# DeltaNet steps: keys, normed output and values turned by VectorE and through memory instead of TensorE; sums of squares by ScalarE

## The reference

```
h = rmsnorm(x);  proj = h @ w_in            # 9232 columns
o_r = retention(rq, rk, rv)                 # 4 heads, chunks of 128
q, k, v = silu(causal_conv(dq, dk, dv))     # 4 taps
o_d = gated_deltanet(l2norm(q), l2norm(k), v, beta, g)   # 8 heads of 128 columns
o_d = o_d * rsqrt(mean(o_d * o_d) + eps) * dn_g;  o_d = o_d * silu(dz)
x = x + (sigmoid(gr) * (o_r @ w_up_r) + sigmoid(gd) * (o_d @ w_up_d)) @ w_o
```

## Time and profile before

| | us |
|---|---|
| median of three executions | 2646.9 |
| span of the profiled execution | 2644.2 |
| TensorE busy | 2620.6 |
| VectorE busy | 1761.1 |
| ScalarE busy | 704.5 |
| GpSimd busy | 798.6 |

### The profile page before, as it was taken

How to read it: one execution, slowest core, us unless ns; L and a number is a source line. 1 busy time by engine, 2 the same in 40 slices (tenths; PEclk the granted TensorE clock), 3 DMA queues, 4 the chain that set the end, 5 groups by cost and what they waited for, 6 DMA issues and landing times.

```text
span 2644.2 us, 40210 instructions
## 1 busy us (share of the span) xinstructions
PE 2620.6 (99%) x14874; PEld 2238.1 (85%) x14874; DVE 1761.1 (67%) x3972; ACT 704.5 (27%) x1440; POOL 798.6 (30%) x451
## 2 busy tenths in 40 slices
PE   8999999999999999999999999999999999999998
PEld 6888888888888899888877888888888998898887
DVE  7878777877755555434577778777877555653333
ACT  5333333333311212200143333333332221231001
POOL 3123333333312212334512233332322122132453
PEclk9999999999999999999999999999999999999999
DMA  5321222122211112433533222222222111133344
GB/s 174 100 85 58 81 69 85 53 86 65 85 50 43 41 35 76 130 96 120 157 90 88 77 74 69 73 77 72 67 77 73 43 51 43 41 106 100 99 135 152
DMA packets 293416, 217.79 MB, mean 82 GB/s; under 512 B 31747, under 2 KB 246101, under 8 KB 292965
## 3 DMA queue, kind: packets, MB, share of 16 engines
q1 hardware_dynamic: 259620, 159.07, 20.9%
q10 hardware_dynamic: 33600, 56.15, 6.3%
HBM read 176.30 MB, written 38.86 MB: 81 GB/s over the span
## 4 chain that ended last, share of the span: by engine, by line
PE 92%; DVE 3%; DMA 2%; issue 1%; ACT 1%; SPq 0%; POOL 0%; ACTq 0%; DVEq 0%; POOLq 0%
PE dense_ps L866 23%; PE dense_ps L870 23%; PE dense_ps L868 23%; PE work L849 3%; PE dense_ps L890 2%; PE dense_ps L891 2%; PE dense_ps L892 2%; PE work L1145 1%; PE work L1182 1%; PE work L1202 1%; PE work L1121 1%; PE work L1104 1%; PE work L1171 1%; PE work L1195 1%; PE work L1156 1%
## 5 line engine op out<-in xcount | busy, mean ns | idle before, releaser
L866 PE MATMUL dense_ps<-act_hi,w_hi 128*128 128x512 f32 x2552 | 1048.3, 411 | 1.7 <-DVE w_lo L1797 0.8
L870 PE MATMUL dense_ps<-act_hi,w_lo 128*128 128x512 f32 x2552 | 998.4, 391 | 0.0
L868 PE MATMUL dense_ps<-act_lo,w_hi 128*128 128x512 f32 x2552 | 997.3, 391 | 0.0
L2579 POOL TENSOR_TENSOR w_lo<-w_raw,w_hi 128x1024 fp32r<-128x1024 f32 x162 | 400.1, 2470 | 1024.5 <-ACT w_hi L1429 582.7
L870 PEld LDWEIGHTS dense_ps<-act_hi,w_lo 128*128 128x128 f32 x2552 | 479.0, 188 | 105.8
L866 PEld LDWEIGHTS dense_ps<-act_hi,w_hi 128*128 128x128 f32 x2552 | 481.0, 188 | 86.9 <-POOL act_lo L2600 2.3
L868 PEld LDWEIGHTS dense_ps<-act_lo,w_hi 128*128 128x128 f32 x2552 | 481.5, 189 | 78.8 <-issue 0.5
L1973 DVE SCALAR_TENSOR_TENSOR arena<-arena,cols 128x512 f32<-128x512 f32 x288 | 244.3, 848 | 6.1
L1429 ACT ACTIVATE w_hi<-w_raw 128x1024 fp32r<-128x1024 f32 x94 | 99.1, 1054 | 330.5 <-PE dense_ps L870 310.5
L1419 ACT ACTIVATE arena<-dense_ps 128x512 f32<-128x512 f32 x96 | 57.2, 596 | 258.5 <-PE dense_ps L870 258.5
L849 PE MATMUL work<-mk,arena 128*128 128x128 f32 x768 | 112.1, 275 | 7.9 <-DMA arena<-in_x 7.9
(11 more groups left out here) (262 smaller groups left out, 4094.7 us busy)
## 6 DMA issues: line engine op xcount, KB each, us to landing
w_raw<-in_w_in SPq DMA_DIRECT2D x138, 512.0 KB, 3.8
arena<-l_scratch SPq DMA_DIRECT2D x64, 256.0 KB
arena<-gate_scratch ACTq DMA_DIRECT2D x64, 256.0 KB, 2.7
gate_scratch<-arena ACTq DMA_DIRECT2D x36, 256.0 KB, 2.0
w_raw<-in_w_out SPq DMA_DIRECT2D x18, 512.0 KB, 3.7
o_scratch<-arena ACTq DMA_DIRECT2D x32, 256.0 KB, 2.2
w_raw<-in_w_up_dn SPq DMA_DIRECT2D x16, 512.0 KB, 3.6
arena<-o_scratch ACTq DMA_DIRECT2D x32, 256.0 KB, 3.7
```

Of the source, the lines that this page charges most:

```text
L866: eng.matmul(dense_ps[:, to, :], w_hi[:, slot, k, :], hi[:, k, seg], start=(k == 0), stop=False)
L868: eng.matmul(dense_ps[:, to, :], w_hi[:, slot, k, :], lo[:, k, seg], start=False, stop=False)
L870: mm = eng.matmul(dense_ps[:, to, :], w_lo[:, slot, k, :], hi[:, k, seg], start=False, stop=(k == KT - 1))
L2579: eng.tensor_tensor(w_lo[:, slot, :, :], w_from[second][:, :, :], w_hi[:, slot, :, :].bitcast(F32), ALU.subtract)\
```

## The change

In the seven even and seven odd units of a layer, TensorE turns neither the normed output nor the values, and in all of them but even units of head 0 not the keys either. VectorE turns blocks of 32x32 within 512 columns instead (`turn_o`, `turn_v`, `turn_k`, slots 15 to 17) into `turned`; ScalarE's queue writes them to memory in four transfers of 32 partitions each (`put_v`, slot 16, `put`, slot 18), so that the blocks of one 128x128 tile come to stand in turned order, and reads them back with tokens on the partitions into `tokens` (`get_v`, slot 19, `get`, slot 21). The values have transfers of their own. The values' product vt moves from slot 19 to slot 23. The gated output of a unit is made in slot 3 of the next one (`late_ob`) and stored in its slot 10 (`late_store`). The keys turned in a unit are those which the next one's kt reads. In odd units of head 6 turn_k does nothing. `turned` and `tokens` lie where the retention later has its rotated keys and queries. The sums of squares of queries and outputs are made by ScalarE's activations with an accumulated output, one for each chunk, and VectorE's two reductions are gone. Some semaphores are joined to make room for the new ones. The core of the diff:

```diff
 HBUF = 4
+BACK = 3
+BACK_O, BACK_K, BACK_V = range(BACK)
...
         at(13, "og")
         if kind.endswith("last"):
             at(16, "ob")
-        at(18, "store")
+            at(18, "store")
+        if kind in ("even", "odd"):
+            at(3, "late_ob")
+            at(10, "late_store")
+        elif kind == "even_last":
+            at(1, "late_ob")
+            at(3, "late_store")
...
-        at(vt, "vt")
+        at(23 if kind in ("even", "odd") else vt, "vt")
...
     if kind in ("even", "odd"):
         at(12, "mask", 1)
         at(14, "dec", 1)
-        begin(15, 1, ("ob",))
+        begin(15, 1, ("turn_o",))
+        at(16, "turn_v")
+        at(16, "put_v")
+        at(19, "get_v")
+        at(17, "turn_k")
+        at(18, "put")
+        at(21, "get")
...
+        turned = arena[:, swap_at:swap_at + BACK * HALF].rearrange("p (m s) -> p m s", s=32)
+        tokens = arena[:, swap_at + BACK * HALF:swap_at + 2 * BACK * HALF].rearrange("p (x c t) -> p x c t", x=BACK, c=CPH)
...
+        back_dram = nc.dram_tensor("back_scratch", [CPH * CPH * BACK, 32, P], F32)
...
                         elif what == "kt":
 
+                            if kind == "odd" or kind == "even" and h:
+                                continue
...
                         elif what == "vt":
 
+                            if kind in ("even", "odd"):
+                                continue
...
                         elif what == "ob":
-                            eng.wait_ge(on_ok.sem, on_ok.after(t, 1))
-                            turn(1 + b, [on[:, c, :] for c in range(CPH)]).then_inc(ob_ps.sem, 1)
+                            eng.wait_ge(on_ok.sem, on_ok.after(t, BACK + 1))
+                            turn(1 + b, [on[:, c, :] for c in range(CPH)]).then_inc(back_ps.sem, 1)
...
-                            if t is not None:
-                                eng.wait_ge(og_s.sem, og_s.after(t, 0))
-                            eng.activation(sq, wk[1 + nb][:, :], ACT.Square).then_inc(sq_ok.sem, 1)
+                            eng.wait_ge(qe_s.sem, qe_s.after(tn, 0))
+                            for c in range(CPH):
+                                ins = eng.activation(sq[:, c * P:(c + 1) * P], wk[1 + nb][:, c * P:(c + 1) * P], ACT.Square,
+                                                     accum_out=qss[:, c:c + 1])
+                            ins.then_inc(sq_ok.sem, 1)
...
                         elif what == "osq":
                             eng.wait_ge(o_ps.sem, o_ps.after(t, CPH))
-                            if kind != "odd_last":
-                                eng.wait_ge(qe_s.sem, qe_s.after(tn, 1))
-                            eng.activation(osq, wk[1 + b][:, :], ACT.Square).then_inc(osq_ok.sem, 1)
+                            eng.wait_ge(og_s.sem, og_s.after(t, 0))
+                            for c in range(CPH):
+                                ins = eng.activation(osq[:, c * P:(c + 1) * P], wk[1 + b][:, c * P:(c + 1) * P], ACT.Square,
+                                                     accum_out=og[:, 0, c:c + 1])
+                            ins.then_inc(osq_ok.sem, 1)
+                        elif what == "put_v":
+                            u = back(l, h, b)
+                            ms = slice(BACK_V * CPH * CPH, (BACK_V + 1) * CPH * CPH)
+                            eng.wait_ge(on_ok.sem, on_ok.after(t, 3))
+                            eng.wait_ge(back_v_in.sem, back_v_in.after(u, 0))
+                            for i in range(CPH):
+                                rows = slice(32 * i, 32 * i + 32)
+                                eng.dma_start(back_dram[ms, :, rows].rearrange("m r s -> r m s"), turned[rows, ms, :])\
+                                   .then_inc(back_v_st.sem, 16)
+                        elif what == "get_v":
+                            u = back(l, h, b)
+                            ms = slice(BACK_V * CPH * CPH, (BACK_V + 1) * CPH * CPH)
+                            eng.wait_ge(back_v_st.sem, back_v_st.after(u, 64))
+                            eng.wait_ge(vb_ok.sem, vb_ok.after(tn, 0))
+                            eng.dma_start(tokens[:, BACK_V], back_dram[ms, :, :].rearrange("(m j) r d -> (j r) m d", j=CPH))\
+                               .then_inc(back_v_in.sem, 16)
+                        elif what == "put":
+                            u = back(l, h, b)
+                            ms = slice(0, 2 * CPH * CPH)
+                            eng.wait_ge(on_ok.sem, on_ok.after(t, BACK + 1))
+                            eng.wait_ge(back_in.sem, back_in.after(u, 0))
+                            for i in range(CPH):
+                                rows = slice(32 * i, 32 * i + 32)
+                                eng.dma_start(back_dram[ms, :, rows].rearrange("m r s -> r m s"), turned[rows, ms, :])\
+                                   .then_inc(back_st.sem, 16)
+                        elif what == "get":
+                            u = back(l, h, b)
+                            eng.wait_ge(back_st.sem, back_st.after(u, 64))
+                            eng.wait_ge(kd_ok.sem, kd_ok.after(tn, 1))
+                            eng.wait_ge(ob_ok.sem, ob_ok.after(t, 0))
+                            eng.dma_start(tokens[:, 0:2].rearrange("p x c t -> p (x c) t"),
+                                          back_dram[0:2 * CPH * CPH, :, :].rearrange("(m j) r d -> (j r) m d", j=CPH))\
+                               .then_inc(back_in.sem, 16)
+                        elif what == "late_store":
+                            if kind == "even" and h == 0:
+                                continue
+                            seg = slice(nb * HALF, (nb + 1) * HALF)
+                            eng.wait_ge(ob_ok.sem, ob_ok.after(t - 1, 1))
+                            eng.dma_start(o_dram[bass.ds(h - nb, 1), :, seg].rearrange("k p t -> p (k t)"), sz[:, seg])\
+                               .then_inc(o_st[nb].sem, 16)
...
+                    elif old is not None and old % (2 * DH) == 0:
+                        eng.wait_ge(back_ps.sem, back_ps.after(l, 1))
                     elif old is not None:
-                        eng.wait_ge(vt_ps.sem, vt_ps.after(old, 1))
+                        eng.wait_ge(on_ok.sem, on_ok.after(old - 1, 3))
...
-                            eng.wait_ge(kt_ps.sem, kt_ps.after(tn, 1))
+                            if kind == "odd" or kind == "even" and h:
+                                eng.wait_ge(back_in.sem, back_in.after(back(l, h, b) - 1, 16))
+                                src = tokens[:, BACK_K]
+                            else:
+                                eng.wait_ge(kt_ps.sem, kt_ps.after(3 * l + ("first", "even", "even_last").index(kind), 1))
+                                src = chunks(4)
...
-                            eng.tensor_tensor(kd[nb], chunks(4), per_token(hs[:, 3, ns_of]), ALU.mult).then_inc(kd_ok.sem, 1)
+                            eng.tensor_tensor(kd[nb], src, per_token(hs[:, 3, ns_of]), ALU.mult).then_inc(kd_ok.sem, 1)
...
-                            eng.tensor_reduce(qss, sq.rearrange("p (c t) -> p c t", c=CPH), mybir.AxisListType.X, ALU.add)\
-                               .then_inc(qe_s.sem, 1)
-                            eng.wait_ge(qe_s.sem, qe_s.after(tn, 1))
...
                         elif what == "vt":
-                            eng.wait_ge(vt_ps.sem, vt_ps.after(tn, 1))
+                            if kind in ("even", "odd"):
+                                eng.wait_ge(back_v_in.sem, back_v_in.after(back(l, h, b), 16))
+                                src = tokens[:, BACK_V]
+                            else:
+                                eng.wait_ge(back_ps.sem, back_ps.after(l, 1 if kind == "first" else 3))
+                                src = chunks(0)
...
                             eng.wait_ge(vs_ok.sem, vs_ok.after(tn, 1))
-                            eng.tensor_tensor(vb[nb], chunks(0), per_token(ky[:, 5, :]), ALU.mult).then_inc(vb_ok.sem, 1)
+                            eng.tensor_tensor(vb[nb], src, per_token(ky[:, 5, :]), ALU.mult).then_inc(vb_ok.sem, 1)
...
-                            eng.tensor_reduce(og[:, 0, :], osq.rearrange("p (c t) -> p c t", c=CPH), mybir.AxisListType.X,
-                                              ALU.add).then_inc(og_s.sem, 1)
-                            eng.wait_ge(og_s.sem, og_s.after(t, 1))
-                            eng.wait_ge(qe_s.sem, qe_s.after(t, 2))
+                            eng.wait_ge(qe_s.sem, qe_s.after(t, 1))
...
+                        elif what == "turn_o":
+                            eng.wait_ge(on_ok.sem, on_ok.after(t, 1))
+                            eng.transpose(turned_of(BACK_O), on.rearrange("p c t -> p (c t)")).then_inc(on_ok.sem, 1)
+                        elif what == "turn_v":
+                            eng.wait_ge(kqv_ok.sem, kqv_ok.after(hn, 5 + nb))
```

(16 more changed lines are left out.)

43 lines of the change are left out of this document (29 added, 14 removed).

## The result

The changed kernel takes 2765.5 us (median of four executions, 2759.2 to 2766.6), the kernel before 2645.6 on the same chip: 1.045 times as long (95% interval 1.044 to 1.046), 120 us more. The forecast was 2665 us with 2687 as its upper end: the sign is right, the size is not. The profiled execution took 2765.3 us and spans 2763.4.

A forecast was written before the change was run, and what follows sets the result against it. TensorE, busy 99%, was taken to bound the kernel. Each pair gained +2.4 us of even-unit lateness less 1.15 saved in the odd unit, +1.3; 14 pairs, +18 on 2646.9, gave 2665 us, forecast's own range 2643 to 2687, overall 2614 to 2687.

The forecast's parts named there:

- the stall at vt: TensorE waits at ks_0 of odd units for vt, moved behind the even unit's last silu: 3.5 us, 14 times.
- rival 1: At the even unit's end VectorE finishes vt in time, so the whole 31.5 us saving shows: 2615 us; chance 0.23.
- the prices on VectorE and ScalarE: Per unit, block turns of 0.69 us on VectorE; sums cost ScalarE 0.8 us more, delaying nothing.
- the first term without a row: A 128x512 block turn on VectorE, a size no profile row showed: 0.69 us, with 0.48 and 1.2 as ends.
- 0.9 us worse off, as reckoned: Even unit's end: GpSimd's later low part holds VectorE's filter taps, +0.9 us (0 to 1.1).
- A turn's price on TensorE: Four transposes: 0.36 us for an output or key turn, 0.43 for a value turn; 31.5 us over both layers.
- SP's chain ... comes 1.8 us later; the solve of the next unit starts 2.4 us later itself.: Weight load, solve's stores and loads, behind GpSimd's low part, come 1.8 us later, covered by the next solve's 2.4 us.
- the 2.3 us that TensorE was to save in a pair: Turns removed from TensorE in an even and an odd unit: 1.15 us in each ordinary unit.
- Rival 2: Small packets cost 31 ns, put lands late, ScalarE stands at get: +81 us, 2728 us; chance 0.12.
- my place for this rival, the tanh: Even unit's end: ScalarE stands at get with the second queries' tanh behind it; vt ends at 676.9, unit grows 5.1 us.

The follow-up runs named there:

- early_even: Whole change, but in even units the values' block turn, stores and load stand in slots 2, 5 and 8, and vt in slot 19: 2720.2 us, 1.028.
- sums_only: Kernel before the change with only the two sums of squares moved to ScalarE: 2646.4 us, 1.000.
- split_first: Changed kernel with put_v one slot later (17), behind ScalarE's weight split: 2753.1 us, 1.040.
- early_even_split: Whole change with the even units' values turned, stored and loaded early, vt there in slot 19, and the odd units' put_v behind the weight split: 2680.2 us, 1.013.
- key_traffic: Kernel with only the output through memory, plus the keys' block turn, stores and load, read by nobody: 2654.0 us, 1.0032.
- values_pe: Changed kernel with the values turned by TensorE again; keys and output still through memory: 2659.3 us, 1.0046.
- key_src_sbuf: Kernel with only the output through memory, with kt's product reading unturned keys in SBUF in 26 units: 2634.3 us, 0.996.
- output_only: Changed kernel with values and keys turned by TensorE; only the normed output through memory, sums on ScalarE: 2632.1 us, 0.994.
- keys_later: Kernel with keys and output through memory, values by TensorE, with the odd units' kt in slot 4 instead of 2: 2658.7 us, 1.005.
- mended_keys_pe: Whole change with keys by TensorE, the even units' values early and the odd units' put_v behind the weight split: 2631.2 us, 0.995.
- mended_v2: mended_keys_pe with the even units' last silu moved behind the odd unit's first uu: 2629.1 us, 0.994.

## Why the prediction was right in sign and wrong in size

**Right: the stall at vt.** Forecast 3.5 us at ks_0 of the odd units, 14 times; measured 48.3 / 14 = 3.45. That vt went "from slot 19 to slot 23, behind that last silu" is its cause: with the even units' values early and vt back in slot 19 it vanishes (early_even), and 45 us with it. This also decides rival 1: VectorE was not in time. The sign isn't luck either: in the pair above the first stall and the clock behind it outweigh all that TensorE saved, by 3.2 us.

**Right: the prices on VectorE and ScalarE.** The block turns, the first term without a row, took what I had chosen between 0.48 and 1.2. The end of the even unit above, VectorE and GpSimd:

```profile
621.30 0.69 DVE L2435 STREAM_TRANSPOSE arena<-arena 128x512 f32<-128x512 f32 x1
...
622.39 4.34 DVE L2051 SCALAR_TENSOR_TENSOR arena<-arena,cols 128x512 f32<-128x512 f32 x3
622.47 2.93 POOL L2693 TENSOR_TENSOR w_lo<-w_raw,w_hi 128x1024 fp32r<-128x1024 f32 x1 [2.80 <-ACT w_hi L1463]
...
630.67 0.69 DVE L2067 SCALAR_TENSOR_TENSOR arena<-arena 128x512 f32<-128x512 f32 x1 [0.69 <-ACT arena L1469]
631.27 0.68 DVE L2322 TENSOR_TENSOR arena<-arena 128x512 f32<-128x512 f32 x1
```

The three taps at 622.39 take 4.34 us beside GpSimd's low part; three of them took 2.33 before (665.21), where one tap of 1.62 stood ahead of them for 0.48, so they are 0.9 us worse off, as reckoned. The last tap ends 27.1 us behind ks_3 where it ended 26.1 behind it before, 1.0 later; I had 0.8. Over the run a tap's mean went from 0.85 to 1.07 us. vt follows the silu without a wait for its rows (over the run 3.1 us in 9 waits): get_v was in time. The sums on ScalarE cost nothing (sums_only). A turn's price on TensorE came out at 0.43 where I had 0.36 for the output's.

**Wrong: "SP's chain ... comes 1.8 us later; the solve of the next unit starts 2.4 us later itself."** This is the step that missed the second stall. It is true for the next unit only if that is an odd one, which has the stall at ks_0 in front of it. For an even unit, behind an odd one without a stall, TensorE comes earlier, not later, and nothing covers the delay. I had walked SP's chain for one kind of unit and let it stand for both. What the runs show in its place is a second stall, 38.2 us in 12 waits and 7.0 in 2 at L1229, with the clock behind it; it goes with put_v behind the split (split_first, early_even_split). The size was short too. Against the next ks_1, the eight stores stand 7.9 us ahead (575.46 to 583.35) where they stood 11.2 ahead before (710.25 to 721.4), 3.3 later; the loads stand 1.1 us ahead (582.27) in place of 6.2 (715.17). Four issues of put_v at 0.4 to 0.5 us were about right: they take 2.0 us in the median, 2.32 in this unit. But I gave the solve's stores no delay from put and put_v, whose packets precede them; they land after 3.4 us and not 2.1. In key_traffic, where a delay of this kind stands alone, it costs 22 us.

**Wrong: the clock had no price.** "The granted clock should stay at its upper level; if stalls lower it, all terms grow" stood under what would show it, and no term or rival had it. In the pair above it adds 1.2 us behind the first stall and 2.7 behind the second; of the growth around the second 0.45 us is not assigned.

**The sum again.** Per pair of the profile above, against before: +3.4 and -0.7 from ks_3 to ks_0 of the odd unit (29.15 against 26.5), +1.2 behind it; -0.7 from ks_3 of the odd unit to ks_1 of the even one; +4.45 and +2.7 around the second stall (3.43 of stall, 0.57 at xu_1, 2.7 clock). That is 10.35, against 98.8 - 88.5 = 10.3. Of the 2.3 us that TensorE was to save in a pair 1.4 can be seen here; in the pairs in which ks_3 of the odd unit to ks_1 of the even one takes 30.24 us (31.57 before) it is 2.1. Fourteen such pairs would be 144 us; but this one is the longest, the fourteen grew by 8.4 us on average, and that makes 117 of the 120.

**Rival 2, small packets, is answered by halves.** The queue that carries the new transfers had this before:

```profile
q10 hardware_dynamic: 33600, 56.15, 6.3%
```

and this after:

```profile
q10 hardware_dynamic: 253120, 100.20, 13.6%
```

These are 219,520 packets more for 3350 us of one engine's time (13.6% of 16 x 2763 less 6.3% of 16 x 2644), 15 ns each; with the forecast's 31 ns for the 43,008 of 512 B that the loads make (28 x 1024 and 28 x 512), about 12 are left for one of 128 B, as taken. ScalarE issued get_v at 573.69, 0.1 us behind put's last store, and didn't stand there; my place for this rival, the tanh, was wrong. But its core, that the burst delays somebody, was right: the one delayed is SP's chain of 4 KB stores.

**Left open.** That the product of the keys, which reads SBUF now, is held is seen (2.07 us at 582.14, 0.69 before), beside GpSimd's low part of 581.27 to 583.65. The Trainium skill (SBUF — State Buffer, Who interferes with whom) says that a VectorE instruction with two SBUF inputs, as this one, contends with a GpSimd instruction that reads SBUF, and that one with a single SBUF input, outside the fast modes, doesn't. The traces agree on both: in values_pe all 26 block turns of the keys lie wholly beside GpSimd's low part and take 0.69 to 0.70 us. The prediction could show that for the taps alone. What the held product costs by itself no run shows: in key_src_sbuf it was held by 0.4 us only. Between values_pe and output_only lie 27 us. key_traffic's 22 us of packets were measured with TensorE still turning the keys; in values_pe it doesn't, which at the forecast's 0.36 saves 9. So 27 + 9 - 22 = 14 us are not assigned. The place where most of them may lie is ks_1 to ks_2 of the odd units, 6.5 us in values_pe against 5.7, in all 11: the keys' product is held there (1.5 us), but keys_later, in which it isn't (0.68), got only 0.3 of the 0.8 us back. Turning the keys early, as the values, wasn't tried.

## What to carry to other kernels

When work is moved to a queue, follow every chain that hangs behind it to its last consumer, and do it for each kind of iteration: cover that a stall gives in one kind is missing in the other. Transfers that nobody waits for still cost if they are issued in a burst right ahead of small ones that somebody does; the same number of bytes in smaller stores and partly at another time was free here. A stall of TensorE is to be priced with the clock behind it, here up to 2.7 us on one of 3.4.

## What the hardware showed that I had not expected

The length of a stall doesn't decide alone whether the clock falls. Behind 3.37 us (533.23) it fell, for about 3.4 us; around the end of 3.43 us (593.50) it was at 0.56 on average for seven. In the same run it fell at a stall of 2.38 us (397.86) and stayed at 1.00 at stalls of 2.47 (1958.31) and 2.94 us (2054.29); in early_even it fell behind 2.46 us. The kernel before has one stall of 2.9 us, in the second layer, and there the clock stayed up too. The three stretches are the one behind 397.86 and the one behind 1958.31, both after, and the one behind 1415.60, before:

```profile
397.86:401.00 3.14, 3.14 (x9) 2.56 (x10) 2.26 (x12) 0.00 (x0) 0.00 (x0) 0.50 0.00 0
1958.31:1962.00 3.69, 3.69 (x22) 3.29 (x23) 2.96 (x14) 0.28 (x1) 0.00 (x0) 1.00 0.00 0
...
1415.00:1417.00 2.00, 1.40 (x7) 1.26 (x8) 1.83 (x10) 0.00 (x0) 0.00 (x0) 1.00 0.02 4
```

The other surprise is how little the three turns cost one by one, and how much they do at one place. The values' way was free with the even units' part early and the odd units' stores behind the split (2631.2 us, all values through memory), the output's way gained 12 us, and the keys' block turn was free; with all of them in slots 16 to 21, 120 us were lost. The reverse holds too: spread, the values' way gave back only 1 us of the 12 that TensorE's rows promise for 28 turns. The steps of mended_keys_pe against those of output_only, on average over the 14 pairs, say where the rest went: ks_3 of an odd unit to ks_1 of the even one is 0.43 us shorter (30.71 against 31.14) and ks_3 of the even unit to ks_0 of the odd one 0.18, but ks_0 to ks_1 of the odd unit is 0.24 longer, which the moved silu of mended_v2 takes back, and ks_1 to ks_2 of the even unit 0.26.
